# Scores and top-16 beside the query products, a second top-16 over 100 sums, and gate one-hots in four operations

## Chip, core and metric

One core of one Trainium2 chip. The time is what one execution takes on the device, in microseconds, as the median of several runs. TensorE (PE) does matrix products, VectorE (DVE), ScalarE (ACT) and GpSimd (POOL) work on vectors, and SyncE (SP) issues most of the transfers. "Us" are microseconds.

## What is computed

Two layers of an encoder on 512 tokens of width 1024. Each has a conv and pooling mixer, and then a retrieval of single-neuron experts (PEER), which is the part that the change touches:

```python
def peer(h, w_q, sub_keys, u_tab, v_tab):
    q = (hf @ w_q).reshape(T, PEER_HEADS, 2, D_HALF)
    s = jnp.einsum("thpd,hpkd->thpk", q, sub_keys)
    top_v, top_i = lax.top_k(s, PEER_TOPK)
    comb = (top_v[:, :, 0, :, None] + top_v[:, :, 1, None, :]).reshape(
        T, PEER_HEADS, PEER_TOPK * PEER_TOPK)
    best_v, best_j = lax.top_k(comb, PEER_TOPK)
    i1 = jnp.take_along_axis(top_i[:, :, 0], best_j // PEER_TOPK, axis=-1)
    i2 = jnp.take_along_axis(top_i[:, :, 1], best_j % PEER_TOPK, axis=-1)
    idx = (i1 * N_KEYS + i2)
    gate = jax.nn.softmax(best_v, axis=-1)
    a = jnp.einsum("tmd,td->tm", u_tab[ib], xb)
    wgt = gb * jax.nn.gelu(a, approximate=False)
    return jnp.einsum("tm,tmd->td", wgt, v_tab[ib])
```

There are 8 heads with 2 halves each (16 segments of 128 scores), top 16 of each, and 16,384 experts. Before each of the two parts of a layer the tokens are normalized and modulated: a shift, a scale and a gate, each a product of a condition vector with a part of `w_ada`, 48 blocks of 128 rows per layer.

## The kernel before

All 16,384 experts are computed densely, in 128 chunks of 128: the **u stage** forms gelu(u h) for each chunk, the **v stage** sums v times the weights, which are zero for experts that a token did not choose. Weights come in tiles of 128 x 1024 f32 (512 KB) into a ring of four slots. Each product is done in three parts of eight matmuls, with the weights split in a high and a low half: ScalarE makes the high half (`hi`), POOL or VectorE the low one (`lo`), TensorE multiplies (`product`). A layer runs: input products, conv and pooling, output products, 16 **query products** (wq), 64 **score** matmuls, 128 u chunks, 128 v chunks.

Beside the u stage VectorE does the **retrieval** for four token tiles of 128 tokens (`a` in 0 to 3): `top16` over the 16 segments of 128 scores, sums of the two halves' 16 x 16 best, `top16` over 8 x 256 sums, and six operations on 8 x 16 x 16 f32 elements that look up the chosen indices by one-hots. `RETRIEVING` = 56 is the u chunk at which ScalarE takes the results (`retrieved`). Eight chunks later the **gate stage** begins, 48 u chunks in which VectorE makes one-hots of 8 tokens per chunk (24 operations of 128 elements, L1369 and L1371) and TensorE 16 short f16 matmuls (L616) that put the gates at their experts.

In layer 0 VectorE also does the next layer's 48 modulations (L1285) in between, in bursts (`next_modulation`), from eight slots (`ada_next`, which lie where the queries were). SyncE fills a slot when `next_used` says that the modulation before has been done. These loads stand in the same queue as the u tiles: after the first eight, four loads precede each round of four u tiles, from round 3 to round 12:

```python
up_rounds(1, NEXT_FROM)
with sp.Fori(0, NEXT_ROUNDS // 2) as q:
    for half in range(2):
        for s in range(RING):
            load_next(q + 1, RING * half + s)
        up_round(2 * q + (NEXT_FROM + half))
```

The 32 later modulations of layer 0 itself are loaded and done beside the mixer and the query products (`load_later`, `modulate_later`).

In `product`, u chunk n waits for the gelu of chunk n - 2, which ScalarE does after the split of chunk n.

## Time and profile before

| | |
|---|---|
| median of 3 runs | 3183.66 us (3183.57 to 3186.3) |
| profiled execution | 3189.15 us, span 3187.3 us |
| TensorE busy | 3091.1 us, 97% |
| VectorE busy | 2457.8 us, 77% |
| ScalarE / POOL busy | 1118.5 / 1185.7 us |
| mean granted TensorE clock | 0.987 of full |
| transfers | 230 GB/s over the span |

The profile is of one execution. A row of the timeline gives the start, the duration, engine, source line, operation and tiles, how many instructions it merges, and in brackets the idle time before it and what ended it. Line numbers are those of the kernel before.

### The profile page before, as it was taken

The page shows a single profiled execution, that of the slowest core. Times are in us where ns is not written, and L with a number is a line of the kernel's source. Part 1 is how long each engine was busy: PE and PEld are TensorE (multiplying, and loading weights), DVE is VectorE, ACT ScalarE, POOL GpSimd, SP SyncE. Part 2 cuts the span into 40 slices and gives each one's busy share as a digit, 9 for nine tenths or more (in the row PEclk, how much of TensorE's full clock was granted, in tenths as well). Part 3 has the DMA queues.
Part 4 walks back from the last instruction along what each step waited for, and adds up shares of the span by engine and source line. Part 5 has one row for each costly group of instructions (what it writes and reads, how often), then busy time and mean ns, then how long its engine had stood idle before and what let it go on. Part 6 is the DMA issues. An engine that isn't in the chain of part 4 may idle for free.

```text
span 3187.3 us, 54768 instructions
## 1 busy us (share of the span) xinstructions
PE 3091.1 (97%) x16200; PEld 2682.7 (84%) x16200; DVE 2457.8 (77%) x5952; ACT 1118.5 (35%) x1590; POOL 1185.7 (37%) x765
## 2 busy tenths in 40 slices
PE   6989999999999999999999999999999999999998
PEld 4668888778888899999975788888788889999997
DVE  7981999859995488999977239951799926889987
ACT  3333322234443333333343332223344433333333
POOL 0033445420001366766700334544000024667674
PEclk8999999999999999999999999999999999999999
DMA  6162666445556799999921224444455578999996
GB/s 254 62 216 101 241 231 240 165 139 188 215 207 256 254 362 361 360 361 363 374 91 40 85 82 142 147 145 141 149 218 210 189 287 293 362 358 361 361 371 238
DMA packets 278481, 734.76 MB, mean 231 GB/s; under 512 B 36064, under 2 KB 118368, under 8 KB 276448
## 3 DMA queue, kind: packets, MB, share of 16 engines
q1 hardware_dynamic: 186688, 462.03, 41.7%
q0 software_dynamic: 50688, 151.18, 12.8%
q10 hardware_dynamic: 40992, 120.34, 9.6%
q8 instruction: 34, 0.56, 0.1%
q14 instruction: 79, 0.65, 0.1%
HBM read 613.85 MB, written 119.54 MB: 230 GB/s over the span
## 4 chain that ended last, share of the span: by engine, by line
PE 54%; POOL 18%; issue 14%; DVE 10%; DMA 2%; ACTq 1%; ACT 1%; DVEq 0%; SPq 0%; POOLq 0%
PE bank L507 30%; PE bank L511 15%; POOL z_pad L934 9%; POOL u_pad L928 5%; PE bank L616 3%; POOL z_pad L928 2%; POOL scratch L928 2%; PE bank L528 2%; DVE scratch L1285 2%; PE bank L427 1%; ACTq L826 1%; DVE h L1266 1%; DVE h L1263 1%; PE bank L451 1%; DVE h L1265 1%
## 5 line engine op out<-in xcount | busy, mean ns | idle before, releaser
L507 PE MATMUL bank<-h_hi,w_hi 128*128 128x512 f32 x2528 | 997.9, 395 | 19.2 <-ACT norm_tmp L807 16.3
L673 ACT ACTIVATE w_hi<-ring 128x1024 fp32r<-128x1024 f32 x584 | 615.0, 1053 | 1116.0 <-PE bank L511 1036.8
L507 PE MATMUL bank<-h_lo,w_hi 128*128 128x512 f32 x2528 | 988.2, 391 | 0.0
L913 POOL TENSOR_TENSOR w_lo<-ring,w_hi 128x1024 fp32r<-128x1024 f32 x172 | 442.8, 2575 | 844.2 <-ACT w_hi L673 844.1
L633 PE MATMUL bank<-v_lo,w_hi 128*128 128x368 f32 x2032 | 670.5, 330 | 0.0
L633 PE MATMUL bank<-v_hi,w_hi 128*128 128x368 f32 x2032 | 665.2, 327 | 2.7 <-DVE v_lo L1439 1.8
L511 PE MATMUL bank<-h_hi,w_lo 128*128 128x512 f32 x2528 | 624.3, 389 | 0.0
L507 PEld LDWEIGHTS bank<-h_hi,w_hi 128*128 128x128 f32 x2528 | 476.9, 189 | 119.4 <-ACT w_hi L673 19.1
L507 PEld LDWEIGHTS bank<-h_lo,w_hi 128*128 128x128 f32 x2528 | 476.7, 189 | 97.1
L511 PEld LDWEIGHTS bank<-h_hi,w_lo 128*128 128x128 f32 x2528 | 474.5, 188 | 98.6
L934 POOL DMA_INDIRECT z_pad<-ga_scratch,z_pad x288 | 374.0, 1299 | 155.0 <-issue 86.9
L1371 DVE TENSOR_SCALAR h<-iota_b,keys 128x128 f16<-128x128 f16 x1536 | 406.6, 306 | 0.0
L633 PEld LDWEIGHTS bank<-v_hi,w_hi 128*128 128x128 f32 x2032 | 381.4, 188 | 4.3 <-DVE v_lo L1439 2.9
L633 PEld LDWEIGHTS bank<-v_lo,w_hi 128*128 128x128 f32 x2032 | 380.7, 187 | 0.1
L637 PE MATMUL bank<-v_hi,w_lo 128*128 128x368 f32 x2032 | 379.8, 329 | 0.0
L1442 DVE TENSOR_TENSOR w_lo<-ring,w_hi 128x1024 fp32r<-128x1024 f32 x256 | 314.2, 1227 | 71.2 <-ACT w_hi L673 66.3
L673 ACT ACTIVATE v_hi<-scratch 128x368 fp32r<-128x368 f32 x256 | 130.9, 512 | 653.0 <-PE bank L637 402.2
L637 PEld LDWEIGHTS bank<-v_hi,w_lo 128*128 128x128 f32 x2032 | 344.7, 188 | 0.0
L928 POOL DMA_INDIRECT h<-v_t,z_pad x8 | 13.0, 1628 | 604.3 <-ACT w_hi L673 603.7
L928 POOL DMA_INDIRECT u_pad<-v_t,z_pad x132 | 167.9, 1272 | 165.5 <-DVE scratch L1391 94.5
L1369 DVE TENSOR_SCALAR h<-iota_b,keys 128x128 f16<-128x128 f16 x768 | 189.5, 247 | 0.0
L1391 DVE SCALAR_TENSOR_TENSOR scratch<-u_pad,z_pad,scratch 128x1024 f32<-128x1024 f32 x132 | 169.3, 1282 | 10.9 <-issue 1.3
(184 smaller groups left out, 2885.0 us busy)
## 6 DMA issues: line engine op xcount, KB each, us to landing
ring<-u_t SPq DMA_DIRECT2D x256, 512.0 KB
ring<-v_t SPq DMA_DIRECT2D x256, 512.0 KB
ga_scratch<-norm_tmp ACTq DMA_DIRECT2D x256, 256.0 KB, 2.0
g_scratch<-scratch ACTq DMA_DIRECT2D x12, 4096.0 KB, 13.8
scratch<-ga_scratch SPq DMA_DIRECT2D x256, 192.0 KB
scratch<-ada_t SPq DMA_DIRECT2D x76, 512.0 KB, 5.8
scratch<-g_scratch SPq DMA_DIRECT2D x32, 768.0 KB
keys<-g_scratch SPq DMA_DIRECT2D x32, 768.0 KB
```

The lines of the kernel that those rows point to most:

```text
L507: pe.matmul(to, w_hi[:, b, k * P:(k + 1) * P], part_h[:, k, :], start=(k == 0 and part_h is h_hi), stop=False)
L511: mm = pe.matmul(to, w_lo[:, b, k * P:(k + 1) * P], h_hi[:, k, :], start=False, stop=(k == KC - 1))
L633: pe.matmul(bank[:, k, 0:TD], w_hi[:, b, k * P:(k + 1) * P], part_w[:, b, 0:TD], start=(first and part_w is v_hi), stop=False)
L637: mm = pe.matmul(bank[:, k, 0:TD], w_lo[:, b, k * P:(k + 1) * P], v_hi[:, b, 0:TD], start=False, stop=False)
L673: return act.activation(to, of, ACT.Copy)
L913: pool.tensor_tensor(w_lo[:, n % 2, :], ring[:, n % RING, :], w_hi[:, n % 2, :].bitcast(F32), ALU.subtract).then_inc(tile_used[n % RING], 1)
L928: pool.indirect_dma_start(to, None, v_rows, bass.IndirectOffsetOnAxis(ap=own_i[:, n:n + 1].bitcast(U32), axis=0))\
L934: pool.indirect_dma_start(own_w[:, n:n + 1], None, ga_cells, bass.IndirectOffsetOnAxis(ap=own_e[:, n:n + 1].bitcast(U32), axis=0))\
L1369: dve.tensor_scalar(hot2[:, b, j, :], iota_b[:, :], i2_t[:, col], None, ALU.is_equal)
L1371: ins = dve.tensor_scalar(hot1[:, b, j, q, :], iota_b[:, :], i1_t[:, col], g_part[:, col], ALU.is_equal, ALU.mult)
L1391: dve.scalar_tensor_tensor(to, own_rows[s], own_w[:, bass.ds(ROWS * n + (EARLY_ROWS + s), 1)], to, ALU.mult, ALU.add).then_inc(rows_used, 1)
L1442: dve.tensor_tensor(w_lo[:, b, :], ring[:, s, :], w_hi[:, b, :].bitcast(F32), ALU.subtract)\
```

## The change

- **Scores.** Instead of after all query products, the four score matmuls of segment s (`score`) stand behind query product s + 2, in PSUM banks 0 and 1 by turns; ScalarE copies segment n - 3 after the query copy n (`copy_score`). The last two segments follow the last product.
- **First top-16.** Done by pairs of segments (8 of 128 elements: 2 segments x 4 token tiles) as they arrive, before any token tile's other work.
- **Second top-16.** Of the 16 x 16 sums only 3 rows of 16 and 13 rows of 4 are formed and searched, 100 per head.
- **Index look-up.** Ranks of both halves in one f16 comparison of 4096 elements, one f16 product, and halving additions in place of two reductions. A step counter gains 8 per token tile.
- **Modulations.** The last 8 of layer 0's own are no longer loaded beside the query products, but into the eight `ada_next` slots when all scores are done (`load_own`), ahead of the next layer's 48; so 56 are done in the retrieval: 5 + 5 + 4 per token tile. Six loads precede each round of four u tiles, from round 1 to round 8.
- **RETRIEVING** goes from 14 to 11 rounds, 56 to 44 chunks; the gate stage starts 12 chunks earlier.
- **Gate one-hots.** Four operations of 1024 elements per chunk in place of 24 of 128. `hot1` holds two tokens interleaved, so TensorE reads it with a step of two elements. The transposed indices and gates are kept in f16.

```diff
     NEXT_SLOTS = 8
-    NEXT_FROM = 3
-    NEXT_ROUNDS = (N_ADA - NEXT_SLOTS) // RING
+    NEXT_FROM, PER_ROUND = 1, 6
+    OWN_ADA = KC
+    N_NEXT = OWN_ADA + N_ADA
+    NEXT_ROUNDS = (N_NEXT - NEXT_SLOTS) // PER_ROUND
     ADA_FIRST = 2 * KC
-    LATER = N_ADA - ADA_FIRST
+    LATER = N_ADA - ADA_FIRST - OWN_ADA
     ADA_EARLY = 2
-    RETRIEVING = 14 * N_U // 32
+    RETRIEVING = 11 * N_U // 32
...
+    SIDE = 2
+    WIDE, NARROW, ROWS_WIDE = 16, 4, 3
+    CANDS = ROWS_WIDE * WIDE + (TOPK - ROWS_WIDE) * NARROW
...
+        hot2 = hb[:, 0:2 * TOK * P].rearrange("p (b j i) -> p b j i", b=2, i=P)
+        hot1 = hb[:, 2 * TOK * P:6 * TOK * P].rearrange("p (b q g i j) -> p b q g i j", b=2, q=2, i=P, j=SIDE)
...
                 def load_next(turn, s):
 
-                    sp.wait_ge(next_used[s], N_ADA // NEXT_SLOTS * l + turn + 1)
-                    sp.dma_start(ada_next[:, s, :], ada_t[(l + 1) % DEPTH, NEXT_SLOTS * turn + s]).then_inc(next_landed[s], 16)
+                    sp.wait_ge(next_used[s], N_NEXT // NEXT_SLOTS * l + turn + 1)
+                    sp.dma_start(ada_next[:, s, :], ada_t[(l + 1) % DEPTH, NEXT_SLOTS * (turn - 1) + s])\
+                      .then_inc(next_landed[s], 16)
+                def load_own(s):
+                    sp.wait_ge(next_used[s], N_NEXT // NEXT_SLOTS * l + 1)
+                    sp.dma_start(ada_next[:, s, :], ada_t[l, N_ADA - OWN_ADA + s]).then_inc(next_landed[s], 16)
 
                 def up_round(r):
                     for s in range(RING):
...
 
                 up_rounds(0, 1)
                 with sp.If(l < LAST):
-                    sp.wait_ge(score_ready, 4 * TT * l + 4 * TT)
+                    sp.wait_ge(score_ready, SEGS * l + SEGS)
                     for s in range(NEXT_SLOTS):
-                        load_next(0 * l, s)
+                        load_own(s)
                     settle(sp)
-                    up_rounds(1, NEXT_FROM)
-                    with sp.Fori(0, NEXT_ROUNDS // 2) as q:
-                        for half in range(2):
-                            for s in range(RING):
-                                load_next(q + 1, RING * half + s)
-                            up_round(2 * q + (NEXT_FROM + half))
+                    with sp.Fori(0, NEXT_ROUNDS // 4) as q:
+                        for half in range(4):
+                            for i in range(PER_ROUND * half, PER_ROUND * (half + 1)):
+                                load_next(3 * q + (i // NEXT_SLOTS + 1), i % NEXT_SLOTS)
+                            up_round(4 * q + (NEXT_FROM + half))
...
+                def score(s):
+                    pe.wait_ge(q_ready, N_WQ * l + (s + 1))
+                    if s >= 2:
+                        pe.wait_ge(score_ready, SEGS * l + (s - 1))
+                    for a in range(TT):
+                        mm = pe.matmul(bank[:, s % 2, a * P:(a + 1) * P], q_t[:, s, a * P:(a + 1) * P], keys_v[:, s, :],
+                                       start=True, stop=True)
+                    mm.then_inc(score_product, 1)
+                pe.wait_ge(keys_landed, 16 * l + 16)
                 for n in range(2, N_WQ):
                     if n >= 6:
 
                         pe.wait_ge(q_ready, N_WQ * l + (n - 6 + 1))
                     product(l, 0, stages["wq"] + n, bank[:, 2 + n % 6, :])
-
-                pe.wait_ge(q_ready, N_WQ * l + N_WQ)
-                pe.wait_ge(keys_landed, 16 * l + 16)
-                for a in range(TT):
-                    if a >= 2:
-                        pe.wait_ge(score_ready, 4 * TT * l + 4 * (a - 1))
-                    for s in range(SEGS):
-                        mm = pe.matmul(bank[:, 4 * (a % 2) + s // 4, (s % 4) * P:(s % 4 + 1) * P],
-                                       q_t[:, s, a * P:(a + 1) * P], keys_v[:, s, :], start=True, stop=True)
-                        if s % 4 == 3:
-                            mm.then_inc(score_product, 1)
+                    score(n - 2)
+                score(N_WQ - 2)
+                score(N_WQ - 1)
...
                         for j in range(TOK):
                             to = bank[:, 2 + 2 * b + j // PER_BANK, (j % PER_BANK) * P:(j % PER_BANK + 1) * P]
+                            g, i = j // SIDE, j % SIDE
                             for q in range(2):
-                                mm = pe.matmul(to, hot2[:, b, j, :], hot1[:, b, j, q, :], start=(q == 0), stop=(q == 1))
+                                mm = pe.matmul(to, hot2[:, b, j, :], hot1[:, b, q, g, :, i], start=(q == 0), stop=(q == 1))
...
+                def copy_score(s):
+                    act.wait_ge(score_product, SEGS * l + (s + 1))
+                    copy(scores[:, :, s, :], bank[:, s % 2, :].rearrange("p (a k) -> p a k", k=P)).then_inc(score_ready, 1)
                 for n in range(N_WQ):
                     hi(0, stages["wq"] + n + 2)
                     copy(q_t[:, n, :], bank[:, 2 + n % 6, :]).then_inc(q_ready, 1)
-                for s in range(LATER_SLOTS):
-                    act.wait_ge(later_used[s], LATER // LATER_SLOTS + 1)
-                for a in range(TT):
-                    for b in range(4):
-                        act.wait_ge(score_product, 4 * TT * l + (4 * a + b + 1))
-                        copy(scores[:, a, 4 * b:4 * b + 4, :],
-                             bank[:, 4 * (a % 2) + b, :].rearrange("p (s k) -> p s k", k=P)).then_inc(score_ready, 1)
+                    if n >= 3:
+                        copy_score(n - 3)
+                for s in range(N_WQ - 3, N_WQ):
+                    copy_score(s)
...
+                PAIR = 2 * TT
+                big_s = big[:, 0:PAIR * P].rearrange("p (s k) -> p s k", k=P)
+                for pair in range(SEGS // 2):
+                    def seg(n):
+                        return 2 * pair + n // TT, n % TT
+                    dve.wait_ge(score_ready, SEGS * l + (2 * pair + 2))
+                    settle(dve)
+                    top16(PAIR, lambda n: scores[:, seg(n)[1], seg(n)[0], :], lambda n: big_s[:, n, :],
+                          lambda n: vals[:, seg(n)[0], seg(n)[1], :], lambda n: idx_u[:, seg(n)[0], seg(n)[1], :])
...
+                    at = ROWS_WIDE * WIDE
+                    count(dve.tensor_tensor(big_c[:, :, 0:at].rearrange("p h (i j) -> p h i j", j=WIDE),
+                                            v2[:, :, 0, 0:ROWS_WIDE].unsqueeze(3).to_broadcast(wide),
+                                            v2[:, :, 1, :].unsqueeze(2).to_broadcast(wide), ALU.add))
+                    link(dve.tensor_tensor(big_c[:, :, at:CANDS].rearrange("p h (i j) -> p h i j", j=NARROW),
+                                           v2[:, :, 0, ROWS_WIDE:TOPK].unsqueeze(3).to_broadcast(narrow),
+                                           v2[:, :, 1, 0:NARROW].unsqueeze(2).to_broadcast(narrow), ALU.add))
                     settle(dve)
                     top16(HEADS, lambda s: big_c[:, s, :], lambda s: sc_c[:, s, :], lambda s: best[:, s, :],
                           lambda s: bj_v[:, s, :])
-                    next_modulation(3 if a < TT - 1 else 2)
-
+                    next_modulation(5)
...
-                    for half, (jf, to) in enumerate(((ja_f, i1_f), (jb_f, i2_f))):
-                        link(dve.tensor_tensor(eq_4, jf.unsqueeze(3).to_broadcast(shape4),
-                                               iota_f[:, :].unsqueeze(1).unsqueeze(1).to_broadcast(shape4), ALU.is_equal))
-                        link(dve.tensor_tensor(eq_4, eq_4, i2[:, :, half, :].unsqueeze(2).to_broadcast(shape4), ALU.mult))
-                        link(dve.tensor_reduce(to[:, a, :].rearrange("p (h k) -> p h k", k=TOPK), eq_4, AX_X, ALU.add))
-                        next_modulation(3 if a < TT - 1 else 2)
+                    count(dve.tensor_scalar(jb_u, bj, 2, None, ALU.logical_shift_right))
+                    count(dve.tensor_copy(idx_h[:, :, :], idx_u[:, :, a, :]))
+                    count(dve.tensor_copy(j_f, bj))
+                    dve.wait_ge(dve_step, STEPS * l + (FIRST + steps[0] - 2))
+                    count(dve.tensor_copy(ja_f, ja_u))
+                    link(dve.tensor_copy(jb_f, jb_u))
+                    link(dve.scalar_tensor_tensor(ja_f, jb_f, float(ROWS_WIDE - at // NARROW), ja_f, ALU.add, ALU.max))
+                    count(dve.tensor_copy(ranks_2[:, :, 0, :], heads(ja_f)))
+                    link(dve.tensor_scalar(j_at, ja_f, float(NARROW), float(at - NARROW * ROWS_WIDE), ALU.mult, ALU.add))
+                    link(dve.scalar_tensor_tensor(j_at, ja_f, float(WIDE), j_at, ALU.mult, ALU.min))
+                    link(dve.tensor_tensor(ranks_2[:, :, 1, :], heads(j_f), heads(j_at), ALU.subtract))
+                    link(dve.tensor_tensor(eq_4, ranks.unsqueeze(2).to_broadcast(shape4),
+                                           iota_rank.unsqueeze(1).to_broadcast(shape4), ALU.is_equal))
+                    link(dve.tensor_tensor(eq_4, eq_4, idx_h.unsqueeze(3).to_broadcast(shape4), ALU.mult))
+                    next_modulation(5)
+                    half = TOPK // 2
+                    while half > 1:
+                        link(dve.tensor_tensor(eq_4[:, :, 0:half, :], eq_4[:, :, 0:half, :], eq_4[:, :, half:2 * half, :],
+                                               ALU.add))
+                        half //= 2
+                    eq_2 = eq_4.rearrange("p (h e) i k -> p h e i k", e=2)
+                    for e, to in enumerate((i1_f, i2_f)):
+                        ins = dve.tensor_tensor(heads(to[:, a, :]), eq_2[:, :, e, 0, :], eq_2[:, :, e, 1, :], ALU.add)
+                        count(ins)
+                    dve.wait_ge(dve_step, STEPS * l + (FIRST + steps[0]))
+                    next_modulation(4)
...
-                        for j in range(TOK):
-                            t = RING * TOK * r + (s * TOK + j)
-                            col = bass.ds(t, 1)
-                            dve.tensor_scalar(hot2[:, b, j, :], iota_b[:, :], i2_t[:, col], None, ALU.is_equal)
-                            for q, g_part in enumerate((ghi_t, glo_t)):
-                                ins = dve.tensor_scalar(hot1[:, b, j, q, :], iota_b[:, :], i1_t[:, col], g_part[:, col],
-                                                        ALU.is_equal, ALU.mult)
-                        ins.then_inc(hot_ready, 1)
+                        cols = bass.ds(RING * TOK * r + s * TOK, TOK)
+                        shape = [P, TOK // SIDE, P, SIDE]
+                        def along(of):
+                            return of[:, cols].rearrange("p (g j) -> p g j", j=SIDE).unsqueeze(2).to_broadcast(shape)
+                        table = iota_side.unsqueeze(1).to_broadcast(shape)
+                        dve.tensor_tensor(hot1[:, b, 1, :, :, :], table, along(i1_t), ALU.is_equal).then_inc(hot_step, 1)
+                        dve.tensor_tensor(hot2[:, b, :, :], iota_b[:, :].unsqueeze(1).to_broadcast([P, TOK, P]),
+                                          i2_t[:, cols].unsqueeze(2).to_broadcast([P, TOK, P]), ALU.is_equal)
+                        dve.wait_ge(hot_step, LATE * l + RING * r + s + 1)
+                        dve.tensor_tensor(hot1[:, b, 0, :, :, :], hot1[:, b, 1, :, :, :], along(ghi_t), ALU.mult)
+                        dve.tensor_tensor(hot1[:, b, 1, :, :, :], hot1[:, b, 1, :, :, :], along(glo_t), ALU.mult)\
+                           .then_inc(hot_ready, 1)
```

How the instructions move. SyncE's queue before, at the end of the eight loads behind round 0 (`ada_t` to `scratch` are the modulation tiles):

```order
L345 ISA [waits next_used7]
L345 DMA scratch<-ada_t 128x1024
L352 UNCONDITIONAL_BRANCH
L352 ISA
L304 ISA [waits tile_used0]
L304 DMA ring<-u_t 128x1024
L304 ISA [waits tile_used1]
L304 DMA ring<-u_t 128x1024
```

SyncE's queue after the change, between the eight own loads and the next u tile (two more pairs, for slots 0 and 1, stand right ahead of it):

```order
L347 ISA [waits next_used2]
L347 DMA scratch<-ada_t 128x1024
L347 ISA [waits next_used3]
L347 DMA scratch<-ada_t 128x1024
L347 ISA [waits next_used4]
L347 DMA scratch<-ada_t 128x1024
L347 ISA [waits next_used5]
L347 DMA scratch<-ada_t 128x1024
L307 ISA
L308 ISA [waits tile_used0]
L308 DMA ring<-u_t 128x1024
```

Here the next u tile stands behind six further modulation loads, each with a wait for a slot, where before it stood right behind the first eight.

VectorE before, from the end of token tile 0's first top-16 (`h` holds values and indices, `u_pad` the copy with the found values struck out):

```order
L1266 MAX_INDEX h<-h,u_pad 128x8 [waits dve_step]
L1266 MAX_INDEX h<-h,u_pad 128x8 x15
L1258 REGISTER_ALU
L1281 COMPARE_AND_BRANCH [waits dve_step]
L1284 ISA
L1285 SCALAR_TENSOR_TENSOR scratch,mod_sum<-scratch,cond 128x1024 [waits next_landed0]
L1285 SCALAR_TENSOR_TENSOR scratch,mod_sum<-scratch,cond 128x1024 [waits next_landed1]
L1285 SCALAR_TENSOR_TENSOR scratch,mod_sum<-scratch,cond 128x1024 [waits next_landed2]
L1285 SCALAR_TENSOR_TENSOR scratch,mod_sum<-scratch,cond 128x1024 [waits next_landed3]
L1281 UNCONDITIONAL_BRANCH
L1298 TENSOR_TENSOR u_pad<-h 128x2048
```

VectorE after the change, from the second top-16 of token tile 0 to the sixth modulation:

```order
L1270 MAX_INDEX h<-h,scratch 128x8 x7
L1262 REGISTER_ALU
L1301 COMPARE_AND_BRANCH [waits dve_step]
L1305 ISA
L1306 SCALAR_TENSOR_TENSOR scratch,mod_sum<-scratch,cond 128x1024 [waits next_landed0]
L1306 SCALAR_TENSOR_TENSOR scratch,mod_sum<-scratch,cond 128x1024 [waits next_landed1]
L1306 SCALAR_TENSOR_TENSOR scratch,mod_sum<-scratch,cond 128x1024 [waits next_landed2]
L1306 SCALAR_TENSOR_TENSOR scratch,mod_sum<-scratch,cond 128x1024 [waits next_landed3]
L1306 SCALAR_TENSOR_TENSOR scratch,mod_sum<-scratch,cond 128x1024 [waits next_landed4]
```

and from there, past the small steps:

```order
L1349 TENSOR_TENSOR z_pad<-u_pad,keys 128x4096 [waits dve_step]
L1084 REGISTER_ALU
L1351 TENSOR_TENSOR z_pad<-z_pad,u_pad 128x4096 [waits dve_step]
L1084 REGISTER_ALU
L1301 COMPARE_AND_BRANCH [waits dve_step]
L1305 ISA
L1306 SCALAR_TENSOR_TENSOR scratch,mod_sum<-scratch,cond 128x1024 [waits next_landed5]
```

The first modulation stood behind the first top-16 of token tile 0 and now stands behind its second; the sixth stands behind the comparison and the product of 4096 elements.

## Rows read from the trace of the kernel before

**Rows 1.** The page: busy time, share of the span, instructions.

```profile
PE 3091.1 (97%) x16200; PEld 2682.7 (84%) x16200; DVE 2457.8 (77%) x5952; ACT 1118.5 (35%) x1590; POOL 1185.7 (37%) x765
```

**Rows 2.** TensorE's waits: us in total, times, longest us.

```profile
PE bank L507 <- ACT norm_tmp L807: 16.3, 3, 6.6
```

**Rows 3.** Timeline of TensorE around layer 1's scores: start us, us.

```profile
1868.24 1.98 PE L511 MATMUL bank<-h_hi,w_lo 128*128 128x512 f32 x8
1873.68 1.97 PE L511 MATMUL bank<-h_hi,w_lo 128*128 128x512 f32 x8
1877.28 14.56 PE L581 MATMUL bank<-keys,scratch 128*128 128x128 f32 x128 [1.63 <-ACT scratch L673]
1893.03 0.49 PE L507 MATMUL bank<-h_hi,w_hi 128*128 128x512 f32 x1 [1.19 <-ACT scratch L673]
```

**Rows 4.** Timeline of ScalarE around layer 0's scores.

```profile
306.75 1.06 ACT L673 ACTIVATE w_hi<-ring 128x1024 fp32r<-128x1024 f32 x1 [3.90 <-PE bank L511]
307.71 0.58 ACT L673 ACTIVATE scratch<-bank 128x512 f32<-128x512 f32 x1
...
322.94 0.60 ACT L673 ACTIVATE scratch<-bank 128x512 f32<-128x512 f32 x1 [0.30 <-PE bank L581]
```

**Rows 5.** Timeline of VectorE, layer 0, from token tile 1 to token tile 2.

```profile
395.70 3.19 DVE L1262 MAX8 h<-scratch 128x8 f32<-128x128 f32 x16 [0.19 <-DVE h L1318]
...
415.59 1.23 DVE L1285 SCALAR_TENSOR_TENSOR scratch<-scratch,cond 128x1024 f32<-128x1024 f32 x1 [0.26 <-DVE h L1266]
...
422.37 2.28 DVE L1298 TENSOR_TENSOR u_pad<-h 128x2048 f32<-128x2048 f32 x1
424.75 2.71 DVE L1262 MAX8 h<-u_pad 128x8 f32<-128x256 f32 x8
...
440.62 2.64 DVE L1285 SCALAR_TENSOR_TENSOR scratch<-scratch,cond 128x1024 f32<-128x1024 f32 x1 [0.26 <-DVE h L1266]
...
477.30 3.19 DVE L1262 MAX8 h<-scratch 128x8 f32<-128x128 f32 x16 [0.19 <-DVE h L1318]
```

**Rows 6.** Timeline of VectorE, token tile 0's look-up, and one subtraction of POOL.

```profile
366.20 0.22 DVE L1306 TENSOR_SCALAR h<-h 128x128 uint32<-128x128 uint32 x1
366.45 0.29 DVE L1307 CAST h<-h 128x256 f32<-128x256 uint32 x1
...
369.38 4.37 DVE L1314 TENSOR_TENSOR z_pad<-z_pad,h 128x2048 f32<-128x2048 f32 x1
...
384.72 2.29 DVE L1314 TENSOR_TENSOR z_pad<-z_pad,h 128x2048 f32<-128x2048 f32 x1
...
391.89 3.41 DVE L1285 SCALAR_TENSOR_TENSOR scratch<-scratch,cond 128x1024 f32<-128x1024 f32 x1
...
390.82 3.39 POOL L913 TENSOR_TENSOR w_lo<-ring,w_hi 128x1024 fp32r<-128x1024 f32 x1 [1.55 <-ACT w_hi L673]
```

**Rows 7.** Timeline of SyncE's issues, layer 0's u stage.

```profile
323.85 4.22 SPq L345 DMA_DIRECT2D scratch<-ada_t  x8
328.51 32.63 SPq L304 DMA_DIRECT2D ring<-u_t  x8
...
558.24 22.28 SPq L345 DMA_DIRECT2D scratch<-ada_t  x4
580.94 19.15 SPq L304 DMA_DIRECT2D ring<-u_t  x7
```

**Rows 8.** Timeline of VectorE, ScalarE and TensorE, then two pieces of the chain.

```profile
578.72 1.23 DVE L1285 SCALAR_TENSOR_TENSOR scratch<-scratch,cond 128x1024 f32<-128x1024 f32 x1 [0.26 <-DVE h L1266]
...
579.87 1.22 DVE L1285 SCALAR_TENSOR_TENSOR scratch<-scratch,cond 128x1024 f32<-128x1024 f32 x1
...
586.90 1.06 ACT L673 ACTIVATE w_hi<-ring 128x1024 fp32r<-128x1024 f32 x1 [10.71 <-DMA ring<-u_t]
...
588.58 0.49 PE L507 MATMUL bank<-h_hi,w_hi 128*128 128x512 f32 x1 [3.09 <-ACT norm_tmp L807]
...
588.58 5.52 PE bank L507 x16
...
601.38 3.63 PE bank L507 x16
```

**Rows 9.** Gate stage of layer 0: us, busy (instructions) by engine, clock, DMA, GB/s.

```profile
707.00:998.00 291.00, 291.00 (x1805) 238.55 (x1805) 272.60 (x1116) 119.05 (x182) 0.66 (x1) 1.00 0.53 197
```

**Rows 10.** The same columns, amid the query products of layer 0.

```profile
250.00:300.00 50.00, 50.00 (x223) 41.38 (x222) 3.47 (x5) 13.89 (x18) 21.99 (x10) 1.00 0.32 106
```

110 lines of the change are left out of this document (50 added, 60 removed).

## Prediction

> **What bounds the kernel now.** I read the busy shares first: TensorE is busy for 97% of the span [rows 1], so time is won or lost only where its stream of products has a hole, or where a product gets longer. Next the waits of TensorE: it stands still for 96 us in all (3187.3 less 3091.1), and one group of these waits concerns the change. Products of the u stage wait 16.3 us behind the gelu of L807, in three pieces [rows 2]. Two of them, of 6.6 us each, come once per layer when ScalarE issues its 24 small DMAs of own_spread; the change leaves those alone. The third is the 3.09 us at 588.58 [rows 8], which the timeline explains, and on which this prediction rests.
>
> Steady state: one product of 24 matmuls takes 5.44 us (1868.24 to 1873.68) [rows 3]. A chunk of the gate stage has 40 matmuls; 1805 of them in 291 us make 45.1 chunks of 6.45 us [rows 9]. TensorE has no hole there, and VectorE is busy 272.6/45.1 = 6.04 us per chunk. So TensorE bounds that stage, by a small margin.
>
> **The hole at 588.58.** SyncE issues u tiles and the next layer's modulation tiles in one queue. In layer 0 it stood in four ada_t issues from 558.24 to 580.52 and only then issued a u tile [rows 7]. What it waited for is VectorE's L1285: the second modulation after the segment work ended at about 579.95, the u tile left at 580.94, ScalarE's split began at 586.90, and TensorE went on at 588.58 [rows 8]. From the end of the modulation that frees the slot to the product is therefore 8.65 us. That is the tightest place of the kernel before (u chunk 48); its first such wait stands before u chunk 12 and costs nothing: eight u tiles after the first four were issued without any of these waits, from 328.51 [rows 7].
>
> **The change, part by part.**
>
> *Scores amid the query products.* Today from the end of the last query product (1873.68 + 1.97) to the first u product (1893.03) are 17.4 us: 1.63 wait, 14.56 of scores, 1.19 wait [rows 3]. Afterwards 13 of the 16 segments lie between products, 0.91 us each plus about 0.1 for the switch (estimate: a gate chunk, 6.45 us, is 24 matmuls in 5.44 and 16 short ones; the last 0.1 is such a switch): 13.1 us. The tail has three segments that wait for ScalarE in turn: split and q copy until 1.6 us after the product (306.75 to 308.29 [rows 4]), then a copy of 0.60 each time [rows 4] with a score product of 0.91 between. That puts the last copy at 4.9 us and the first u product at 5.2. Sum 18.3, so +1.0 us per layer, **+2.0**. ScalarE's added 0.6 us per product hides in a product of 5.44.
>
> *First top-16 during the query products.* VectorE has room: 3.47 us busy of 50 [rows 10]. Sixteen segments of 128 took 19.89 us (395.70 to 415.59) [rows 5]; five steps with about 0.1 us of wait each leave 1.21 us a segment, so a pair (8 segments) takes 10.2. Pairs come every 2 x 6.45 = 12.9 us, but the end is bunched. With t the end of the last query product, scores of pair 5 are there at t - 4.2, of pair 6 at t + 2.6, of pair 7 at t + 4.9. VectorE ends pair 5 at t + 6.1, pair 6 at t + 16.3, pair 7 at t + 26.6: **21.4 us after the first u product starts** (T = t + 5.2).
>
> *Second top-16 over 100 sums.* Eight rows of 256 took 15.87 us (424.75 to 440.62) [rows 5], 1.92 each. Between 1.21 at 128 and 1.92 at 256 the slope gives 1.06 at 100: 9.0 us, which is 6.9 less. The two additions have 800 elements against 2048 in 2.28 [rows 5]: about 1.2 with their waits. VectorE saves this off TensorE's path, so it is worth nothing by itself.
>
> *One-hots of the ranks.* The small steps number 11 and one table copy, at 0.22 to 0.29 each [rows 6]: 3.0. Comparison and product run on 4096 f16 elements each. No row shows an f16 operation on two tensors. Upper bound is the f32 rate, 2.29 us for 2048 [rows 6], so 4.4 each; lower bound half of it, 2.3 each. I take 6.7 for the two together, halfway; the folding additions (2048, 1024, 512, 2 x 128) take 3.7, halfway between 2.8 and 4.7. The Trainium skill ("VectorE: DVE Perf Modes", on what auto-detection checks) says that a two-tensor operation gives two results per cycle only if every operand is 16-bit with step 1; the product's second operand repeats each element with step 0. By it the comparison would take 2.3, the product 4.4 and the additions 2.8, the whole sum coming out 0.9 us per token tile shorter. No run here shows it.
>
> *SyncE's queue.* This is the part that counts. The own third of modulation (8 tiles) now fills all eight slots when the scores are done, and u round 1 (chunks 4 to 7) stands behind six further loads, each of which waits for a modulation. So u tile 4 is issued only after **six modulations**. Before, twelve u tiles were out before the first such wait. When are six done? From T: pair 7 ends 21.4; additions 1.2; top-16 9.0; five modulations at 1.15 (start to start, 578.72 to 579.87 [rows 8]) with branch 6.1; small steps 3.0; comparison and product 6.7; the sixth modulation 1.5. Sum T + 48.9. With the 8.65 of above TensorE resumes at T + 57.55. It runs dry after four products, at T + 21.8. **Hole: 35.7 us.** POOL's subtractions cannot delay VectorE here, since they run dry too.
>
> *The later waits.* Round r needs 6r modulations. A token tile costs VectorE 40.8 us: 1.2 + 9.0 + 14 modulations 17.0 + 2.7 + 6.7 + 3.7 + 0.5. POOL adds to it: the same operation took 4.37 or 2.29 us, the modulation 3.41 while POOL's subtraction ran [rows 6]. In the tile from 395.70 to 477.30 [rows 5] the parts sum to 69.6 and it took 81.6, so 12.0 over 33.8 us of such operations, or 0.355 each; here 11.3 over 31.8, tile 52. The last wait (48 modulations, chunk 32): 21.4 + 43 (first tile, mostly unblocked) + 104 + 33.5 (six modulations in the fourth) + 8.65 = 210.6, against 32 x 5.44 = 174.1: 36.5 us. So the waits end at **36.5**, nearly all of it in the first hole. The waits between need less (rounds 2 to 7: 20 to 31).
>
> *Clock.* Sixteen matmuls after the 3.09 hole took 5.52 us against 3.63 [rows 8], 1.9 lost; I let the new hole lose the same, so this cancels against the hole removed.
>
> *RETRIEVING 14 to 11.* The four tiles end by about T + 221; ScalarE asks for them at chunk 44, T + 239 + 36. No wait, and the last layer has no modulations. The stage only changes its place: 0.
>
> *Gate one-hots.* VectorE drops from 24 operations a chunk to 4 of 1024 elements: at most 4 x 1.22 + 1.22 = 6.1 us with the split, below 6.45. TensorE does the same 16 short matmuls, so 0.
>
> *Sum:* +2.0 + 36.5 - 3.1 = **+35.4 us**. The profiled execution took 3189.15 us (span 3187.3) and would take 3224.6; it lies 5.5 above the median of the three runs, 3183.66, so the forecast is **3219**.
>
> **Rivals.**
>
> *f16 passes at the f32 rate.* Then a token tile takes 56.2 and the last wait decides: 21.4 + 46.5 + 112.4 + 36.3 + 8.65 - 174.1 = 51 us. For it: the f32 rate is the only one in the rows; against it: nothing but the width of the data. Time 3183.7 + 50 = 3234. Chance 0.15.
>
> *Gate product with interleaved one-hots.* TensorE now reads the moving operand with a step of two elements. If that halves its rate, 16 matmuls of a chunk (about 0.9 us of 6.45 [rows 9]) cost 0.9 more, x 96 = +84, time 3303. No row shows a stepped operand. Chance 0.04.
>
> *Faster: the first round is not held.* If the six slots were free for SyncE by T + 13 (21.8 less 8.65), no hole opens. The 3.1 and the 1.9 of clock fall away, and if VectorE's 6.04 us a chunk does hold TensorE in the gate stage, up to 6.45 - 6.31 (40 matmuls without the switch) = 0.14 x 96 = 13 us more; with +2.0: 3168. The point is where the sixth modulation ends; the queue's listing and 35 us of work ahead of it speak against it. Chance 0.05. A version of it in which the first top-16 keeps pace, so that only 10 us are left at T, gives +24, 3208: 0.10.
>
> **How the numbers follow.** Main case 0.66 (3212 to 3227). The range takes in the quick top-16 and the slow f16 passes: 3206 to 3240; outside are 0.05 below, 0.04 above and some of each case's tail. A measurement here can tell 0.2% (6.4 us) from no change. Slower by more: 0.93; within: 0.02; faster: 0.05.
>
> **What would show it.** In the after's timeline of SyncE, six ada_t issues that end some 48 us after the first u product, and u tiles behind them; among TensorE's waits, one of about 36 us in layer 0 at the fifth u chunk, none at 588; in layer 1 no such wait; gate chunks still 6.45 us; 18 us from last query product's work to u. It would be wrong if u tile 4 left in time, if a second hole of over 5 us stood near chunk 32, or if gate chunks were longer.

## The result, and the profile after

The changed kernel takes 3235.03 us (median of 4 runs, 3234.25 to 3236.41), the kernel before 3183.61 beside it (4 runs): a ratio of 1.0162, 95% interval 1.0144 to 1.0179. Forecast were 3219 us, in 3206 to 3240. The direction and the place were right, and the size was 16 us short.

The profiled execution took 3234.25 us, span 3232.4, 45.1 more than the span profiled before. That one lay 5.5 above its median, which is why the medians are 51 apart and the two profiles 45.

Busy time, from the page of the changed kernel:

```profile
PE 3093.1 (96%) x16200; PEld 2685.0 (83%) x16200; DVE 2236.3 (69%) x4122; ACT 1115.7 (35%) x1590; POOL 1141.4 (35%) x741
```

Against [rows 1] TensorE does the same work in the same 3.09 ms. VectorE lost 221 us of work and the kernel became slower: what VectorE saved was not on the path. TensorE's waits of the changed kernel (us in total, times, longest):

```profile
PE bank L514 <- ACT norm_tmp L820: 58.2, 6, 34.9
```

That is 41.9 more than its counterpart in [rows 2]. The timeline of TensorE has the six pieces, here the four that are new and the first of the two that were there before, one per layer, while ScalarE issues its 24 small transfers (`own_spread`):

```profile
380.88 0.79 PE L514 MATMUL bank<-h_hi,w_hi 128*128 128x512 f32 x1 [34.90 <-ACT norm_tmp L820]
...
471.89 0.49 PE L514 MATMUL bank<-h_hi,w_hi 128*128 128x512 f32 x1 [1.53 <-ACT norm_tmp L820]
...
496.11 0.49 PE L514 MATMUL bank<-h_hi,w_hi 128*128 128x512 f32 x1 [1.93 <-ACT norm_tmp L820]
...
546.52 0.79 PE L514 MATMUL bank<-h_hi,w_hi 128*128 128x512 f32 x1 [6.59 <-ACT norm_tmp L820]
...
679.36 0.79 PE L514 MATMUL bank<-h_hi,w_hi 128*128 128x512 f32 x1 [6.65 <-ACT norm_tmp L820]
```

The u stage starts at T = 323.93. The first hole is at the fifth chunk, and the last new one (546.52) before chunk 32, at the round that needs 48 modulations. SyncE's timeline shows why: behind eight own loads come six further ones that end at 373.71, and only then the u tiles of round 1.

```profile
323.66 4.19 SPq L353 DMA_DIRECT2D scratch<-ada_t  x8
358.21 15.50 SPq L347 DMA_DIRECT2D scratch<-ada_t  x6
374.12 2.26 SPq L308 DMA_DIRECT2D ring<-u_t  x4
...
517.81 22.29 SPq L347 DMA_DIRECT2D scratch<-ada_t  x6
```

And VectorE, from the start of token tile 0's sums to its sixth modulation:

```profile
345.68 0.56 DVE L1323 TENSOR_TENSOR u_pad<-h 128x384 f32<-128x384 f32 x1
...
356.57 1.23 DVE L1306 SCALAR_TENSOR_TENSOR scratch<-scratch,cond 128x1024 f32<-128x1024 f32 x1 [0.28 <-DVE h L1270]
...
364.88 2.29 DVE L1349 TENSOR_TENSOR z_pad<-u_pad,keys 128x4096 f16<-128x4096 f16 x1
367.21 4.43 DVE L1351 TENSOR_TENSOR z_pad<-z_pad,u_pad 128x4096 f16<-128x4096 f16 x1
371.90 1.23 DVE L1306 SCALAR_TENSOR_TENSOR scratch<-scratch,cond 128x1024 f32<-128x1024 f32 x1 [0.26 <-DVE z_pad L1351]
```

The sixth modulation ended at 373.13, T + 49.2. ScalarE took the tile up at 379.21, and TensorE went on at 380.88, 7.75 after the modulation.

**Does it add up?** New holes 34.90 + 1.53 + 1.93 + 6.59 = 44.95, less the 3.09 of [rows 8] that is gone: 41.9. Behind a hole TensorE runs for a while at the lower of its two clock levels (granted clock 0.50 of full from 380.9 to 385, 1.00 from 385.5), one matmul per 0.43 us in place of 0.23. The first 16 matmuls took 5.90 us behind the hole of 34.9 (380.88 to 386.78) and 6.64 behind that of 6.59 (546.52 to 553.16), against 3.63 undisturbed: 2.3 + 3.0 lost, some 0.8 behind the two short holes, less 1.9 before. 41.9 + 4.2 = 46.1 us. Layer 0's u stage, from its first matmul to the third part of its last chunk, took 804.66 us for 758.15 before, 46.5 more.

The other stretches differ by little, and both ways. Layer 0's u stage starts 0.15 us earlier; layer 1's takes 0.75 longer (753.56 for 752.81), nearly all through its gate chunks; from layer 0's last u chunk to layer 1's first the changed kernel takes 1.5 less, and 0.5 less behind layer 1's last. That gives the 45.1 between the spans. The last two differences can't be told from chance: the first of these stretches varies from 809.0 to 813.8 us over the nine profiled kernels that are alike in it.

### The profile page after: what moved, and what is told of

The parts are those of the page before. It is cut to its first block, busy times and chain, and to the rows that moved or that the text cites. A ratio compares the mean times of both kernels' runs of the same rounds, so it can differ in the third digit from the quotient of the medians.

```text
span 3232.4 us, 51155 instructions
## 1 busy us (share of the span) xinstructions
PE 3093.1 (96%) x16200; PEld 2685.0 (83%) x16200; DVE 2236.3 (69%) x4122; ACT 1115.7 (35%) x1590; POOL 1141.4 (35%) x741
## 4 chain that ended last, share of the span: by engine, by line
PE 56%; POOL 19%; issue 14%; DVE 8%; DMA 2%; ACTq 1%; ACT 1%; DVEq 0%; SPq 0%; POOLq 0%
PE bank L514 31%; PE bank L518 15%; POOL z_pad L947 9%; POOL u_pad L941 5%; PE bank L627 3%; POOL z_pad L941 2%; POOL scratch L941 2%; DVE scratch L1306 2%; PE bank L535 2%; PE bank L434 1%; ACTq L839 1%; PE bank L458 1%; PE bank L582 1%; DVE z_pad L1351 1%; DVE h L1019 1%
## 5 line engine op out<-in xcount | busy, mean ns | idle before, releaser
L926 POOL TENSOR_TENSOR w_lo<-ring,w_hi 128x1024 fp32r<-128x1024 f32 x148 | 389.3, 2633 | 812.3 <-ACT w_hi L684 812.2
L1495 DVE TENSOR_TENSOR w_lo<-ring,w_hi 128x1024 fp32r<-128x1024 f32 x256 | 314.4, 1228 | 72.3 <-ACT w_hi L684 72.2
L1408 DVE TENSOR_TENSOR w_lo<-ring,w_hi 128x1024 fp32r<-128x1024 f32 x96 | 117.7, 1226 | 256.5 <-ACT w_hi L684 256.5
L941 POOL DMA_INDIRECT u_pad<-v_t,z_pad x132 | 174.4, 1321 | 164.0 <-DVE scratch L1444 92.9
L1465 DVE TENSOR_TENSOR w_lo<-ring,w_hi 128x1024 fp32r<-128x1024 f32 x56 | 68.7, 1226 | 236.2 <-ACT w_hi L684 236.2
```

The costliest lines, as they stand in the source:

```text
L926: pool.tensor_tensor(w_lo[:, n % 2, :], ring[:, n % RING, :], w_hi[:, n % 2, :].bitcast(F32), ALU.subtract).then_inc(tile_used[n % RING], 1)
L941: pool.indirect_dma_start(to, None, v_rows, bass.IndirectOffsetOnAxis(ap=own_i[:, n:n + 1].bitcast(U32), axis=0))\
L1408: dve.tensor_tensor(w_lo[:, b, :], ring[:, s, :], w_hi[:, b, :].bitcast(F32), ALU.subtract)\
L1495: dve.tensor_tensor(w_lo[:, b, :], ring[:, s, :], w_hi[:, b, :].bitcast(F32), ALU.subtract)\
```

## The experiments

The **queue theory** says that the time is lost because SyncE issues u tiles behind modulation loads whose slots VectorE has not freed. The rivals: the gate stage costs something (TensorE's operand with a step of two, or VectorE), or the loss lies in the retrieval's order of work, and goes with the first wait.

### The same change, with the loads further back

Twelve u tiles (eight in the second kernel) after the first four go out before the first further load:

```diff
-    NEXT_FROM, PER_ROUND = 1, 6
+    NEXT_FROM, PER_ROUND = 4, 6      (3 in the second kernel)
                         load_own(s)
                     settle(sp)
+                    up_rounds(1, NEXT_FROM)
```

> The changed kernel with one difference: the six modulation loads per round stand ahead of u rounds 4 to 11 and not 1 to 8 (three u rounds are issued straight behind the own loads). Theory 1 (the holes come from u tiles that stand in SyncE's queue behind loads that wait for modulations): six modulations are done at T + 49 and are now asked for before chunk 16 (T + 87); the 48th, at T + 216 in the changed kernel, comes some 8 us later as POOL runs through, and is asked for before chunk 44 (T + 239), with 8 us from its end to the product. No hole at the fifth u chunk and none over 3 us later; 45 us of holes and their clock losses go, and so does the 3.1 + 1.9 of the kernel before: about 3179 us, a little faster than before. Rival (the holes come from the other parts: VectorE and POOL in each other's way, or tiles late for lack of bandwidth): holes of 20 us or more remain in the u stage of layer 0, 3205 or more.

Measured 3191.76 us (12 runs, 3186.29 to 3194.32), 1.0020 of the kernel before, 1.0012 to 1.0029. The hole of 34.9 is gone and with it 43 of the 51 us: the queue theory holds. The forecast 3179 was missed, though. Apart from the small transfers' hole TensorE's timeline has one in this u stage, before chunk 44, and SyncE's shows the loads that end late:

```profile
567.70 0.79 PE L515 MATMUL bank<-h_hi,w_hi 128*128 128x512 f32 x1 [4.52 <-ACT norm_tmp L821]
```

```profile
536.75 23.75 SPq L347 DMA_DIRECT2D scratch<-ada_t  x6
```

The 48th modulation ended 12 us later than I had taken (T + 236.4 for T + 224). Nearly all of it arose in token tile 0, which took 64.0 us for 44.3 in the changed kernel (the two behind it took as long as there). POOL now subtracts beside VectorE in that tile too, and VectorE waited 5.0 us for its ninth and tenth modulation tile, 4.34 of it here:

```profile
390.03 1.22 DVE L1307 SCALAR_TENSOR_TENSOR scratch<-scratch,cond 128x1024 f32<-128x1024 f32 x1 [4.34 <-DMA scratch<-ada_t]
```

> As before this one, but the modulation loads stand ahead of u rounds 3 to 10. Theory 1: the first wait (six modulations before chunk 12, T + 65) is met; the last (48 modulations before chunk 40, T + 218) is missed by 8 to 15 us, with 2 us of clock: 3188 to 3196. Rival (only the first round's wait costs): no hole, same time as the run from round 4.

Measured 3202.35 us (6 runs), 1.0054, 1.0042 to 1.0066, above the 3188 to 3196 expected: holes of 1.91, 3.02 and 7.68 us. One round earlier costs 10.6 us, a further two 32.7.

### Six modulations first

```diff
                     settle(dve)
+                    if a == 0:
+                        next_modulation(6)
                     top16(HEADS, ...)
-                    next_modulation(5)
+                    if a > 0:
+                        next_modulation(5)
```

(and 4 for 5 at the next place of token tile 0.)

> The changed kernel with the first six modulations done ahead of the second top-16 of token tile 0 (then 4 and 4 in that token tile, so 14 as ever). The sixth ends at about T + 30 instead of T + 49, so the first hole falls from 34.9 to about 16 us. Theory 2 (what the change costs in the end is set by the 48th modulation, which VectorE reaches at the same time whatever is first): later holes grow by what the first loses, the sum stays near 45 us, 3232 to 3240. Rival, which is how the prediction had it (the first hole carries the cost): 3216.

Measured 3234.83 us (4 runs), 1.0152, 1.0137 to 1.0166: no gain at all, though the first hole halved. The timeline of its TensorE:

```profile
361.83 0.79 PE L514 MATMUL bank<-h_hi,w_hi 128*128 128x512 f32 x1 [16.98 <-ACT norm_tmp L820]
...
397.84 0.79 PE L514 MATMUL bank<-h_hi,w_hi 128*128 128x512 f32 x1 [11.66 <-ACT norm_tmp L820]
...
470.94 0.79 PE L514 MATMUL bank<-h_hi,w_hi 128*128 128x512 f32 x1 [5.36 <-ACT norm_tmp L820]
...
543.93 0.58 PE L514 MATMUL bank<-h_hi,w_hi 128*128 128x512 f32 x1 [5.09 <-ACT norm_tmp L820]
```

With one of 0.5 the holes sum to 39.6 us for 44.95, but four of them are long ones, and the lower clock behind each costs another 1.7 to 2.6 us. What was saved at the first wait came back at the next ones: where the u stage ends up is set by when the 48th modulation is done, T + 213.6 here and T + 215.6 in the changed kernel, as the prediction had it. Layer 0's u stage is only 1.7 us shorter (802.94).

### The gate one-hots alone

The kernel before with only the four gate operations, the interleaved `hot1` and TensorE's stepped read of it.

> The kernel before with only the gate one-hots of the change (four operations of 1024 elements per chunk, pairs of tokens interleaved, f16 indices and gates). Theory: TensorE bounds the gate stage, chunks stay at 6.45 us with VectorE's busy time falling from 6.0 to about 4.5 us per chunk: 3183 within 3 us. Rival (VectorE holds TensorE in that stage): up to 0.14 x 96 = 13 us faster, 3170. Rival (stepped moving operand is slower): slower by 20 or more.

Measured 3185.56 us (12 runs), ratio 1.0003, 0.9994 to 1.0011. The gate stage of this kernel and then of the kernel before, by windows (us; PE, PEld, DVE, ACT and POOL busy, clock):

```profile
707.00:998.00 291.00, 291.00 (x1803) 239.37 (x1802) 181.63 (x217) 118.42 (x180) 2.89 (x2) 1.00 0.53 194
```

```profile
707.00:998.00 291.00, 291.00 (x1805) 238.55 (x1805) 272.60 (x1116) 119.05 (x182) 0.66 (x1) 1.00 0.53 197
```

VectorE does a third less and TensorE the same matmuls, two fewer, in the same time. VectorE was not the bound there at 6.04 us a chunk. The stepped operand costs next to nothing: a gate chunk takes 6.460 us for 6.447, which is 0.6 per layer (layer 1's u stage takes 753.43 for 752.81) and 1.3 in all, too little to show in the medians. All runs with the new gate stage have 6.460, all others 6.447. So both parts of this rival fall as causes of the 51 us.

### POOL's part: one sixteenth of the subtraction

POOL subtracts 64 of the 1024 columns of each tile in the first 52 u chunks. This leaves out 15 of 16 columns of the low half, so it is no version of the kernel; it shows what POOL costs VectorE.

```diff
-                with pool.Fori(N_WIN // RING + 1, (stages["u"] + EARLY) // RING) as r:
+                with pool.Fori(N_WIN // RING + 1, stages["u"] // RING) as r:
                     for s in range(RING):
                         lo(r, s)
+                with pool.Fori(stages["u"] // RING, (stages["u"] + EARLY) // RING) as r:
+                    for n in range(RING):
+                        wait_hi(pool, l, r, n)
+                        pool.tensor_tensor(w_lo[:, n % 2, 0:64], ring[:, n % RING, 0:64],
+                                           w_hi[:, n % 2, 0:64].bitcast(F32), ALU.subtract).then_inc(tile_used[n % RING], 1)
```

> The changed kernel, in which POOL subtracts only 64 of the 1024 columns of a tile in the first 52 u chunks of each layer (the other low halves there are left out, so the output is not the reference's). POOL is then busy for some 0.3 us per chunk and not 2.4. Theory 3 (the term mis-sized in the prediction is how much POOL delays VectorE: token tiles of 57 to 59 us where 52 were forecast and 41 is their undisturbed sum): token tiles fall to 40 to 43 us, the first hole stays at 34 to 35 (POOL is idle there anyway), the holes of 1.5, 1.9 and 6.6 us go: about 10 us of holes and 6 of clock less than the changed kernel, 3216 to 3222. Rival (the later holes come from modulation tiles that arrive late, or from VectorE's own steps): token tiles stay over 50 us and the time within 3 us of the changed kernel's.

Measured 3218.21 us (4 runs), 1.0102, 1.0087 to 1.0118, as expected. The first hole stays, at 34.59 us, since POOL stands still there in both kernels, and every later new one is gone. Of the 15.9 us between the two profiled spans (3216.5 and 3232.4) 14.5 lie in layer 0's u stage (790.20 for 804.66), by holes (10.4) and clock; 1.2 lie ahead of it, where the edit changes nothing. Token tiles now start at 344.49, 384.86 and 425.42, 40.4 and 40.6 us apart, against 44.3, 59.1 and 56.8 in the changed kernel; the third takes 46.9, of which VectorE, now ahead of the queue, waits 6.9 for modulation tiles. The same operation in the two kernels, token tile 1, the short one with POOL's part small (first) and the long one of the changed kernel:

```profile
405.93 4.43 DVE L1356 TENSOR_TENSOR z_pad<-z_pad,u_pad 128x4096 f16<-128x4096 f16 x1
```

```profile
417.90 6.50 DVE L1351 TENSOR_TENSOR z_pad<-z_pad,u_pad 128x4096 f16<-128x4096 f16 x1
...
428.82 3.40 DVE L1306 SCALAR_TENSOR_TENSOR scratch<-scratch,cond 128x1024 f32<-128x1024 f32 x1
432.15 1.22 DVE L1306 SCALAR_TENSOR_TENSOR scratch<-scratch,cond 128x1024 f32<-128x1024 f32 x1
```

### Late loads in the kernel before

`NEXT_FROM` 4 for 3, nothing else.

> The kernel before with its modulation loads ahead of u rounds 4 to 13 and not 3 to 12. Theory 1: its only such hole, 3.1 us before chunk 48 (and 1.9 of clock), goes, since the wait moves 21.8 us later: 3180. Rival (that hole has another cause): same as before.

Measured 3194.97 us (11 runs), 1.0029, 1.0020 to 1.0038: slower by 10, where I had expected 5 less. This miss taught the other side of the rule. Its timelines of VectorE, of ScalarE and of TensorE:

```profile
388.80 1.23 DVE L1285 SCALAR_TENSOR_TENSOR scratch<-scratch,cond 128x1024 f32<-128x1024 f32 x1 [11.46 <-DMA scratch<-ada_t]
...
408.49 1.47 DVE L1285 SCALAR_TENSOR_TENSOR scratch<-scratch,cond 128x1024 f32<-128x1024 f32 x1 [2.81 <-DMA scratch<-ada_t]
```

```profile
645.14 0.63 ACT L817 ACTIVATE h<-h 128x512 f32<-128x512 f32 x1 [13.24 <-DVE h L1318]
```

```profile
648.75 0.79 PE L507 MATMUL bank<-h_hi,w_hi 128*128 128x512 f32 x1 [9.52 <-ACT norm_tmp L807]
```

VectorE does the modulations in the middle of the retrieval and waits for their tiles in order. With later loads it stood still for 14.3 us, the retrieval ended late, ScalarE waited 13.24 us for it at chunk 56, and TensorE 9.52 before chunk 58. So the loads have a place from both sides: too early and u tiles stand behind them, too late and the retrieval does.

### Later still, with the results taken at chunk 56

The changed kernel with the loads ahead of rounds 6 to 13 and `RETRIEVING` at 14 rounds again.

> The changed kernel with the loads ahead of u rounds 6 to 13 and RETRIEVING back at 14 rounds. The last wait comes before chunk 52, T + 283, where the 48th modulation is done at T + 237 in the run from round 4: no hole in the u stage of layer 0 but the one of 6.6 us that ScalarE's small DMAs make. Theory 1: 3180, as the kernel before without its 3.1 us hole; everything else that the change does is worth nothing by itself, since it takes work off VectorE alone. Rival (the changed scores, top-16, look-up or gate one-hots cost or save time of their own): differs from the run of the kernel before from round 4 by over 4 us.

Measured 3190.81 us (11 runs), 1.0017, 1.0008 to 1.0026; the forecast 3180 was missed, in part for the same reason. Row one is VectorE's wait for the ninth modulation tile, row two TensorE's hole before chunk 52:

```profile
431.92 1.23 DVE L1307 SCALAR_TENSOR_TENSOR scratch<-scratch,cond 128x1024 f32<-128x1024 f32 x1 [45.66 <-DMA scratch<-ada_t]
```

```profile
610.15 0.49 PE L515 MATMUL bank<-h_hi,w_hi 128*128 128x512 f32 x1 [2.87 <-ACT norm_tmp L821]
```

VectorE stood still 45.7 us, so its 48th modulation ended at 602.62, 42.7 us later than with the loads at rounds 4 to 11 (559.93), and the round that needs it had moved back by 8 chunks, 43.5 us. Nothing was won. This does not explain the whole miss: the hole and the clock behind it cost 4.75 us, the like of the kernel before 4.99, and the gate chunks 1.3, yet the median is 6.0 above. Some 5 us of it stay open, as do some 3 of the 6.8 of the run with the loads from round 4 (hole and clock 7.1); the intervals reach from 2.5 to 8 and from 4 to 9 us.

### ScalarE's 24 small transfers, spread

```diff
                 for r in range(RETRIEVING // RING, EARLY // RING):
                     for s in range(RING):
                         hi(r, stages["u"] + s + 2)
                         gelu(r, s)
+                        n = RING * r + s - RETRIEVING
+                        if n >= 2:
+                            (four of the 24 own_spread transfers)
```

> As the run from round 6 with RETRIEVING 14, and ScalarE issues the 24 small DMAs of own_spread four at a time behind the gelus of six chunks, from the third after the exponential, where they stood together behind the eighth. Each hole of 6.6 us per layer (and some 2.3 of clock) should go, as ScalarE has 3.8 us free per chunk: 3162, faster than both kernels. Rival (the rows of the extra token arrive late, or the DMA issues disturb the splits): the holes come back elsewhere, 3175 or more.

Measured 3171.58 us (5 runs), 0.9953, 0.9939 to 0.9966: 19.2 us below the kernel without the edit, about as much as was expected of it (18). It is above the 3162 because the kernel that it was made from was above its own forecast; its hole before chunk 52 is of 3.54 us. It beats the kernel before, and the question is whether the change has a share in that.

> The kernel before with only the 24 small own_spread transfers of ScalarE spread over six chunks, four behind each gelu. Theory (the gain of the spread transfers is theirs alone, about 13 us of holes and 6 us of lowered clock behind them, and has nothing to do with the change): the 6.6 us hole of each layer goes, the 3.1 us one before chunk 48 stays, 3184.9 less 18 to 20 = 3165 to 3167, and so faster than the changed kernel with the same edit and late loads (3171.6). Rival (the spread transfers pay only beside the shorter retrieval, where ScalarE and VectorE have room at that place): 3178 or more.

Measured 3164.81 us (5 runs, 3163.02 to 3170.69), 0.9945, 0.9931 to 0.9959, beside 3182.71 for the kernel before. It has no share: the same edit on the kernel before gives 17.9 us and is as fast as anything here.

### The change at its best

Loads ahead of rounds 4 to 11, results taken at chunk 48, transfers spread, and in the last token tile 6 + 5 + 3 modulations:

```diff
-                    next_modulation(5)
+                    next_modulation(5 if a < TT - 1 else 6)
...
-                    next_modulation(4)
+                    next_modulation(4 if a < TT - 1 else 3)
```

> The changed kernel with the loads ahead of the rounds 4 to 11, retrieval results taken at chunk 48 instead of 44, the spread own_spread transfers, and in the last token tile six modulations ahead of the look-up instead of five (6 + 5 + 3), so that the 48th, which ended at T + 237 with the loads at these rounds, ends before the look-up's product. Theory (only the queue's two-sided schedule cost time): the hole of 4.5 us before chunk 44 goes, VectorE waits about 4 us for loads, no hole over 2 us is left in the u stage of either layer, 3191.8 - 19 - 4.5 = 3166 to 3169. Rival (something else of the change still costs a few us, since the variant with one hole of 4.5 stood 7 above the kernel before although that has a hole of 3.1): 3172 to 3176.

Measured 3167.11 us (5 runs, 3161.66 to 3170.1), 0.9947, 0.9934 to 0.9961. Windows of layer 0's u stage up to the gates, columns as above:

```profile
324.00:581.00 257.00, 257.00 (x1135) 212.86 (x1135) 243.81 (x580) 72.57 (x94) 134.29 (x47) 1.00 0.73 259
581.00:690.00 109.00, 109.00 (x593) 90.08 (x592) 56.56 (x78) 40.77 (x57) 22.73 (x11) 1.00 0.48 165
```

TensorE is busy for all 366 us, so all holes are closed, and the time still equals that of the kernel before with spread transfers: their intervals overlap nearly whole. A better order makes the change harmless. The median is 2.3 us longer, while the profiled execution is 1.8 shorter (span 3165.4 for 3167.2): layer 0's u stage takes 744.9 for 746.8, as the kernel before still has a hole of 2.19 before chunk 48, and layer 1's 745.0 for 744.3, through the gate chunks. With intervals 4 us wide to each side, no difference between the two is shown. The scores' new place, the second top-16 over 100 sums and the look-up were not run each by itself; this run shows that together they neither cost nor gain more than these few us.

### Without the overlap

```diff
-                    dve.wait_ge(score_ready, SEGS * l + (2 * pair + 2))
+                    dve.wait_ge(score_ready, SEGS * l + SEGS)
```

> The changed kernel with the first top-16 of all pairs held until all scores are copied, so that nothing of it lies beside the query products. It tells what the overlap itself is worth. Theory (the sixth modulation holds the first hole, and VectorE's top-16 of 8 pairs is 8 x 10.2 = 82 us of serial work instead of the 21.6 left at T): sixth modulation at about T + 110, first hole 35 + 61 = 96 us, time 3235 + 58 to 62 = 3293 to 3297. Rival (the overlap is not what counts since POOL's subtractions then stand still and VectorE runs undisturbed, and the later holes shrink by as much as the first grows): 3235 + 45 or less, 3280 or less.

Measured 3294.35 us (4 runs), 1.0349, 1.0333 to 1.0365, 59 above the changed kernel. Its TensorE at the fifth u chunk:

```profile
441.99 0.79 PE L514 MATMUL bank<-h_hi,w_hi 128*128 128x512 f32 x1 [95.81 <-ACT norm_tmp L820]
```

The overlap does move the retrieval 60 us forward: without it token tile 0 starts at 407.26, with it at 345.68. It only shortens a wait that the same change brings in.

## Why the prediction was right, and where it fell short

- **SyncE's queue: right.** Sixth modulation T + 49.2 for T + 48.9; first hole 34.90 us for 35.7; TensorE back 7.75 us after the modulation for 8.65, as the u tile was in ScalarE's hands 5.1 us after its issue (374.12 to 379.21) and not 6.0 [rows 7, 8]. One reading of the rows was off without harm: the modulation that ended at 579.95 is the first after the segment work and not the second (578.72 + 1.23), the 40th in all, and round 12 of the kernel before needs 40.
- **First top-16: right.** Pair 7 ended at T + 21.7 (345.68, with the sums' start) for T + 21.4.
- **The later waits: mis-sized, and the main error of mechanism.** The step "token tile 52, 11.3 of it by POOL" measured 59.1 and 56.8, with 40.4 undisturbed (40.8 forecast). So POOL cost 16.4 to 18.7 us a tile. Most delays are of 1.8 to 2.2 us (4.43 to 6.50, 1.22 to 3.40), nearly the whole of POOL's 2.4 us subtraction. The Trainium skill says the same ("SBUF — State Buffer", on the two sides of SBUF): GpSimd and a VectorE operation with two SBUF inputs share a port pair as an exclusive lock, and whichever starts second is blocked for the other's whole instruction.

  My rate of 0.355 us per us of such work came from a tile in which it filled 33.8 of 69.6 us. In the new tile it fills 31.8 of 40.8, so a subtraction, one per 5.44 us whatever VectorE does, meets such an operation more often: at least 8 of 10 or 11 delayed one in each of the two tiles, 6 of 15 in the tile of [rows 5]. I had scaled by the operations; what comes at a fixed pace is the subtraction. By the lock rule at most one delay of 2.18 per subtraction, 10 to 11 in 57 us, is possible, which is 23; I could have had that as the upper end.

  What the prediction puts at 36.5 is how late chunk 32 starts; it started 48.4 us late (546.52 is T + 222.6, undisturbed T + 174.2), 11.9 more. The two tiles alone are 11.9 (115.9 for 104); what is left cancels, +1.8 in token tile 0 and the parts around the tiles, -1.6 as TensorE restarts 7.0 us after the modulation and not 8.65. The 48.4 are 44.95 of holes and 3.4 of clock.
- **Clock: mis-sized.** I let the losses cancel; there were two long holes (2.3 and 3.0) and two short ones (0.8) for one of 1.9: 4.2 more, of which the 1.1 behind chunk 32 come on top of the 11.9.
- **Scores: mis-sized the other way.** +2.0 forecast; the u stage starts 0.15 us earlier than before, so nothing or a little less than nothing was measured. The tail behind the last query product was placed right: 5.4 us (318.54 to 323.93) for 5.2. Between products a segment costs 0.91 us (310.21 to 316.56 is 6.35, less 5.44) and nothing for a switch, where I had put 0.1: 13 times 0.1 are 1.3 us per layer too much, less the 0.2 of the longer tail. TensorE there, the two last query products' ends and the scores:

```profile
310.21 1.98 PE L518 MATMUL bank<-h_hi,w_lo 128*128 128x512 f32 x8
...
316.56 1.98 PE L518 MATMUL bank<-h_hi,w_lo 128*128 128x512 f32 x8
318.37 1.05 PE L582 MATMUL bank<-keys,scratch 128*128 128x128 f32 x8
320.74 2.02 PE L582 MATMUL bank<-keys,scratch 128*128 128x128 f32 x16 [1.32 <-ACT scratch L684]
323.93 0.49 PE L514 MATMUL bank<-h_hi,w_hi 128*128 128x512 f32 x1 [1.16 <-ACT scratch L684]
```

- **One-hots of the ranks: right in sum, with luck.** 2.29 + 4.43 = 6.72 for 6.7. I had taken the middle of two bounds; one operation was at the lower bound and the other at the upper. **RETRIEVING: right**, 0. **Gate one-hots:** 0 forecast, 1.3 measured (96 chunks, 0.013 us each).
- **Sum.** 35.4 + 11.9 + 1.1 - 2.15 + 1.3 = 47.6, against 45.1 measured; 2.0 of the difference are the stretches behind the two u stages, and 0.55 the small transfers of layer 0, which cost less than before (8.3 us for 8.8, with their clock). So the forecast of the span was 9.7 short. The rest of the 16 is the profiled execution of before: I took its 5.5 off the new kernel too, and the new kernel's profiled execution lay at its median, 0.8 below it. That the measured time is inside the range owes something to the range's upper end, which was set for another reason, the slow f16 passes.
- **Rivals.** "f16 passes at the f32 rate" gave 3234, nearly the measured time, for a wrong reason: only the product ran at that rate (4.43), the comparison took half (2.29), and its token tiles of 56.2 came about through POOL, since they take 40.4 when POOL's part is small. That the time fits is no proof of a mechanism. The stepped operand (0.013 us a chunk for 0.9) and the two faster ones fell.

## What to carry to other kernels

When one in-order queue feeds two consumers at different paces, give every load two dates: after it, the other consumer's tiles wait for this one's slots; before it, this consumer waits for its tile. Work them out for the whole sequence, since easing the first wait only moved the loss to the next ones (3235 for 3235), and shifting the whole block of loads by three rounds gave back 43 us. An operation saved on an engine off the path is worth nothing until a wait on it ends earlier: 221 us less of VectorE, and 211 less in the best order, gave no gain. And before tuning the large stages, look at the small transfers that an engine on the path issues one by one: spreading 24 of them over six chunks was worth 19 us on the changed kernel and 18 on the one before.
